# Expert outputs scattered into a table in token order, and the combination in the expert phase

## The reference, cut to what matters

```python
def hier_moe(h, w_rg, b_rg, w_re, b_re, w_up, w_down):
    ...
    top_v, top_i = lax.top_k(logit_e, TOP_K)
    gate = jax.nn.softmax(top_v, axis=-1) * p_grp
    expert = (grp[:, None] * EXPERTS_PER_GROUP + top_i).reshape(-1)
    ...
    def expert_block(args):
        xb, e = args
        g, u = jnp.split(xb @ w_up[e], 2, axis=-1)
        return (jax.nn.silu(g) * u) @ w_down[e]

    y = lax.map(expert_block, (buf.reshape(n_blocks, MOE_BLOCK, D), blk_expert)).reshape(-1, D)
    y = y[dest] * gate.reshape(-1)[order][:, None].astype(h.dtype)
    return jax.ops.segment_sum(y, tok_sorted, num_segments=n_tok)
```

## Time and profile before

| | us |
|---|---|
| median of 3 runs | 2901.03 |
| lowest and highest run | 2896.57, 2902.46 |
| the profiled execution's own time | 2889.24 |
| its span, first to last instruction | 2887.4 |
| TensorE busy in it | 2759.5 |
| VectorE, ScalarE, GpSimd busy in it | 1506.3, 777.0, 79.0 |

### The profile page before, as it was taken

One profiled execution on the slowest core, in us unless ns is written; L12 is line 12 of the kernel. 1 busy time (PEld: TensorE's weight loads), 2 busy tenths in 40 slices (PEclk: granted clock), 3 DMA queues, 4 the chain that ended last, 5 costly groups with the idle time before them and its releaser, 6 DMA issues. The chain is left out here.

```text
span 2887.4 us, 44114 instructions
## 1 busy us (share of the span) xinstructions
PE 2759.5 (96%) x18251; PEld 1644.2 (57%) x18251; DVE 1506.3 (52%) x2115; ACT 777.0 (27%) x1444; POOL 79.0 (3%) x106
## 2 busy tenths in 40 slices
PE   8999889999999999999999989999998899999985
PEld 4444554444444444444454445656564899999974
DVE  7886676566666668773642008856765111111103
ACT  2111771111111115412100016756423121112111
POOL 0000000000000000000000000000000000000022
PEclk9999999999999999999999999999999899999997
DMA  3022842111111127763231000022202999999992
GB/s 143 31 73 40 264 175 73 44 44 44 44 44 44 44 67 280 265 245 111 71 90 44 8 11 1 1 59 88 75 7 75 375 402 406 409 410 405 405 359 79
DMA packets 82614, 422.65 MB, mean 146 GB/s; under 512 B 13504, under 2 KB 23232, under 8 KB 66496
## 3 DMA queue, kind: packets, MB, share of 16 engines
q1 hardware_dynamic: 58528, 362.29, 34.1%
q10 hardware_dynamic: 15664, 41.95, 4.0%
q0 software_dynamic: 8304, 16.79, 1.8%
HBM read 393.07 MB, written 51.38 MB: 154 GB/s over the span
## 5 line engine op out<-in xcount | busy, mean ns | idle before, releaser
L3605 PE MATMUL ex_up_ps<-big,ex_xT 128*32 128x128 f32 x3072 | 349.1, 274 | 0.0
L3603 PE MATMUL ex_up_ps<-big,ex_xT 128*32 128x384 f32 x3072 | 344.8, 490 | 0.7 <-ACT ex_xT L3690 0.6
L3605 PEld LDWEIGHTS ex_up_ps<-big,ex_xT 128*32 128x32 f32 x3072 | 334.3, 110 | 0.6
L1758 PE MATMUL ffn_ps<-h,V 128*128 128x512 f32 x504 | 219.7, 592 | 0.0
L2217 PE MATMUL ffn_ps<-big,V 128*128 128x512 f32 x484 | 211.3, 597 | 3.7 <-DVE V L2472 1.4
L3603 PE MATMUL ex_y_ps<-ex_wd,ex_hT 128*32 128x384 f32 x1536 | 180.9, 493 | 5.1 <-issue 4.3
L296 DVE TENSOR_SCALAR_CACHE_REDUCE h<-ad_s_ps 128x1280 f32<-128x1280 f32 x64 | 92.9, 1489 | 172.7 <-PE ad_s_ps L205 172.7
L3605 PE MATMUL ex_y_ps<-ex_wd,ex_hT 128*32 128x128 f32 x1536 | 178.8, 276 | 3.0 <-issue 2.9
L3605 PEld LDWEIGHTS ex_y_ps<-ex_wd,ex_hT 128*32 128x32 f32 x1536 | 169.0, 111 | 7.2 <-issue 6.5
L1758 PEld LDWEIGHTS ffn_ps<-h,V 128*128 128x128 f32 x504 | 95.8, 190 | 120.5 <-issue 120.5
L2217 PEld LDWEIGHTS ffn_ps<-big,V 128*128 128x128 f32 x484 | 92.2, 191 | 120.4 <-issue 114.5
(11 more groups left out here) (603 smaller groups left out, 4799.0 us busy)
## 6 DMA issues: line engine op xcount, KB each, us to landing
big<-in_w_eup SPq DMA_DIRECT2D x64, 2048.0 KB, 20.9
ex_wd<-in_w_edown SPq DMA_DIRECT2D x32, 2048.0 KB, 20.7
V<-in_w_down SPq DMA_DIRECT2D x35, 704.0 KB, 5.6
dn_tail<-in_w_mod ACTq DMA_DIRECT2D x48, 512.0 KB, 5.4
fm_up<-in_w_up SPq DMA_DIRECT2D x22, 1028.0 KB, 4.9
y_dram<-in_cos SPq DMA_DIRECT2D x1, 21504.0 KB, 71.5
y_dram<-big ACTq DMA_DIRECT2D x32, 288.0 KB
dn_tail<-in_w_in SPq DMA_DIRECT2D x17, 512.0 KB, 4.6
```

Source lines behind the costliest of these rows:

```text
L1758: mm = nc.tensor.matmul(bank(i, j), wj[:, k, :], bj[:, k, :], start=(k == 0), stop=(k == 3))
L3603: nc.tensor.matmul(o[32 * g:32 * g + 32, 0:W], rows(g), w[:, 0:W], start=first, stop=last)
L3605: mm = nc.tensor.matmul(o[BR:P, g * P:(g + 1) * P], rows(g), w[:, W:BANK], start=first and g == 0, stop=last and g == GR - 1)
```

## The change

`y_dram` becomes a table of 2T = 2048 rows in token order: half 0 holds for each token the row of its expert with the lower number, half 1 the other. The fill of `y_dram` and ScalarE's wait for it go. In the routing, VectorE makes for each row its place in the table (`code`, five instructions, and one more for the ids), and `early`, `late` and their eleven instructions go.

In the expert loop the two stores of a block become three DMAs from SBUF to SBUF on ScalarE's queue (32 KB each), which bring the last 256 columns beside the others, and one indirect DMA on GpSimd's queue, which scatters the 96 rows of 4 KB into the table. GpSimd waits for the three, issues the scatter, and waits for the scatter before it goes on; `keep_y` waits for GpSimd's count `y_free`. The scatters of pair i-1 stand behind the two gathers in iteration i.

At the end there are no gathers: SyncE loads the table as 16 plain tiles of 512 KB, half 0 once the scatter of the last block but one is done, half 1 once the last is. The combination is part of the same phase. Four tiles go through TensorE as before, for the other four ScalarE scales the first expert's rows, and VectorE adds them to the residual, which it makes from the rows that the routing left in `V` times their root mean square (`std`). VectorE makes the gates at the start of the expert phase (`weigh`, ten instructions; the gates are exchanged where the halves are).

```diff
@@ dilated_attention
-                sp.dma_start(y_dram.rearrange("(b p) n -> p b n", p=P),
-                             din["cos2"].unsqueeze(1).to_broadcast([P, NB * BR // P, T])).then_inc(y_filled, 16)
@@ route, VectorE
+                st.done(V_.tensor_tensor(swapped, first_at, c1, ALU.is_gt))
+                for a in range(2):
+                    st.done(V_.tensor_scalar(code[:, a], swapped, float(T) * (1 - 2 * a), float(T) * (a - 2), ALU.mult, ALU.add))
+                    st.done(V_.tensor_tensor(code[:, a], code[:, a], cst["token"], ALU.add))
...
-                V_.tensor_scalar(r["ids"][0:BR, 0:NB], ids_ps[0:BR], float(T), None, ALU.add).then_inc(ids_kept, 1)
+                st.done(V_.tensor_scalar(flag[0:BR], ids_ps[0:BR], -float(T), -float(T), ALU.is_ge, ALU.mult))
+                V_.scalar_tensor_tensor(out=r["ids"][0:BR, 0:NB], in0=ids_ps[0:BR], scalar=2.0 * T, in1=flag[0:BR], op0=ALU.add,
+                                        op1=ALU.add).then_inc(ids_kept, 1)
+                V_.tensor_scalar(r["rows"][0:BR, :], ids_ps[0:BR], 2.0 * T, None, ALU.add)
@@ experts, SyncE
+                for f, got, a in ((f0, got0, 0), (f1, got1, 1)):
+                    sp.wait_ge(up_done, pairs * 2 + (a + 1))
+                    sp.wait_ge(y_free, pairs * 2 + (a + 1))
+                    for t in (4, 0, 5, 1, 6, 2, 7, 3) if a == 0 else range(TT):
+                        sp.dma_start(f[:, t, :], y_dram[a * T + t * P:a * T + (t + 1) * P, :]).then_inc(got[t], 16)
...
@@ experts, GpSimd
+                def scatter(i, u):
+                    nc.gpsimd.tensor_copy(row_at[0:BR, u:u + 1], r["rows"][0:BR, bass.ds(i * 2 + u, 1)]).then_inc(row_set, 1)
+                    pool.wait_ge(row_set, i * 2 + (u + 2))
+                    pool.sem_inc(pool_seen, 1)
+                    pool.wait_ge(moved[u], i * (16 * GR) + 16 * GR)
+                    pool.sem_inc(pool_seen, 1)
+                    pool.indirect_dma_start(y_dram, bass.IndirectOffsetOnAxis(ap=row_at[0:BR, u:u + 1], axis=0), y[0:BR, u, :], None,
+                                            bounds_check=2 * T - 1, oob_is_err=False).then_inc(stored[u], 16)
+                    pool.wait_ge(stored[u], i * 16 + 16)
+                    pool.sem_inc(y_free, 1)
...
                         pool.wait_ge(turned, i * 2 + 1)
                         gather(i, 1, i * 2)
                         pool.wait_ge(turned, i * 2 + 2)
                         gather(i + 1, 0, i * 2 + 1)
+                        scatter(i - 1, 0)
+                        scatter(i - 1, 1)
...
-                        pool.indirect_dma_start(f[:, t, a, :], None, y_rows,
-                                                bass.IndirectOffsetOnAxis(ap=r["early"][:, a, t:t + 1], axis=0),
-                                                bounds_check=NB * BR - 1, oob_is_err=False).then_inc(got[t], 16)
+                scatter(pairs - 1, 0)
+                scatter(pairs - 1, 1)
@@ experts, TensorE, behind down(pairs - 1, 1)
+                token_sum(0)
+                token_sum(1)
+                token_sum(2)
+                pe.wait_ge(y_kept, pairs * 2 + 1)
+                token_sum(3)
@@ experts, ScalarE
-                    act.dma_start(dst[:, 0:2 * W], y[0:BR, u]).then_inc(stored[u], 16)
-                    act.dma_start(dst[:, 2 * W:D].rearrange("(g p) n -> p g n", g=GR),
-                                  y[BR:P, u].rearrange("p (g n) -> p g n", g=GR)).then_inc(stored[u], 16)
+                    for g in range(GR):
+                        act.dma_start(y[32 * g:32 * g + 32, u, 2 * W:D], y[BR:P, u, g * 2 * P:(g + 1) * 2 * P]).then_inc(moved[u], 16)
...
+                for t in range(PET, TT):
+                    act.wait_ge(got0[t], 16)
+                    nc.scalar.activation(f0[:, t, :], f0[:, t, :], ACT.Copy, scale=r["gate"][:, 0, t:t + 1]).then_inc(scaled, 1)
@@ experts, VectorE
                 def keep_y(i, u):
                     dve.wait_ge(y_done, i * 2 + (u + 3))
-                    dve.wait_ge(stored[u], i * (16 * PARTS) + 16 * PARTS)
+                    dve.wait_ge(y_free, i * 2 + (u + 1))
...
+                for t in range(PET, TT):
+                    dve.wait_ge(scaled, t - PET + 1)
+                    row = rows[:, t % ROWS, :]
+                    nc.vector.scalar_tensor_tensor(out=row, in0=row, scalar=r["std"][:, t:t + 1], in1=f0[:, t, :], op0=ALU.mult,
+                                                   op1=ALU.add).then_inc(added, 1)
```

More of the change, by code:

```diff
@@ L3161, in route @@
         g4b, begun = carve(TT, 4), carve(E_)
-        c1, low, pg = (carve(TT) for _ in range(3))
+        c1, low, pg, first_at = (carve(TT) for _ in range(4))
+        code = carve(2, TT)
+        std, swapped = r["std"], r["swapped"]
         base, nblk, incl, onesr, total = (carve(E_) for _ in range(5))
@@ L3461, in _ @@
                                              ALU.is_equal))
-                    st.done(V_.scalar_tensor_tensor(out=here, in0=wide(cst["token"], NB), scalar=-float(T), in1=here,
-                                                    op0=ALU.add, op1=ALU.mult))
+                    st.done(V_.tensor_tensor(here, wide(code[:, a], NB), here, ALU.mult))
                     V_.tensor_tensor(lanes[:, a * TT:(a + 1) * TT, 0:BR], wide(lanef[:, a], BR),
@@ L3520, in experts, with used_pairs @@
             "y_kept"))
+        gates_ready, summed, scaled, added, mixed, squared, rooted, inverted, finished, step = (ph.sem(x) for x in (
+            "gates_ready", "summed", "scaled", "added", "mixed", "squared", "rooted", "inverted", "finished", "step"))
         def used(eng):
             return eng.value_load(r["count"][0:1, 0:1], min_val=1, max_val=NB)
+        def used_pairs(eng):
+            return eng.value_load(r["count"][0:1, 1:2], min_val=1, max_val=NB // 2)
         with nc.Block() as block:
@@ L3552, in _ @@
                         load_down(i, 0, i * 2)
-                pairs = sp.value_load(r["count"][0:1, 1:2], min_val=1, max_val=NB // 2)
+                pairs = used_pairs(sp)
                 load_down(pairs - 1, 1, pairs * 2 - 1)
+                for f, got, a in ((f0, got0, 0), (f1, got1, 1)):
[3 more added lines that the diff above has]
+                        sp.dma_start(f[:, t, :], y_dram[a * T + t * P:a * T + (t + 1) * P, :]).then_inc(got[t], 16)
+                for t in range(TT):
+                    sp.wait_ge(finished, t + 1)
+                    sp.dma_start(out[t * P:(t + 1) * P, :], f1[:, t, :]).then_inc(out_stored, 16)
+                sp.wait_ge(out_stored, 16 * TT)
             @block.gpsimd
@@ L3651, in down, with token_sum @@
                     mm.then_inc(y_done, 1)
+                def token_sum(t):
+                    for k in range(KD):
+                        nc.tensor.matmul(sum_ps[t][:, k // 4, k % 4 * P:(k % 4 + 1) * P], h[:, k, t * P:(t + 1) * P], cst["ident"],
+                                         start=(k % 4 == 0), stop=False)
+                    pe.wait_ge(got0[t], 16)
+                    for half in range(2):
+                        mm = nc.tensor.matmul(sum_ps[t][:, half, :], r["diag"][:, t, :], f0[:, t, half * BANK:(half + 1) * BANK],
+                                              start=False, stop=True)
+                    mm.then_inc(summed, 1)
                 turn(0, 0)
@@ L3777, in _ @@
                         keep_y(i, 0)
[L3778 removed]
+                pairs = used_pairs(dve)
                 keep_hidden(pairs - 1, 1)
@@ new lines, in _ @@
+                for t in range(PET, TT):
[3 more added lines that the diff above has]
+                                                   op1=ALU.add).then_inc(added, 1)
+                def mix(t):
+                    if t < PET:
+                        dve.wait_ge(summed, t + 1)
+                        rest = sum_ps[t].rearrange("p a n -> p (a n)")
+                    else:
+                        dve.wait_ge(added, t - PET + 1)
+                        rest = rows[:, t % ROWS, :]
+                    dve.wait_ge(got1[t], 16)
+                    nc.vector.scalar_tensor_tensor(out=f1[:, t, :], in0=f1[:, t, :], scalar=r["gate"][:, 1, t:t + 1], in1=rest,
+                                                   op0=ALU.mult, op1=ALU.add).then_inc(mixed, 1)
@@ L3913, in experts_block @@
         x_ready = [nc.alloc_semaphore("x_ready0"), nc.alloc_semaphore("x_ready1")]
-        f = big[:, 0:16, :].rearrange("p (t a) n -> p t a n", a=2)
-        got = [nc.alloc_semaphore(f"got{t}") for t in range(TT)]
         with nc.sbuf_tensor("wb", [P, KD, 2 * P], F32) as wb:
```

219 lines of the change are left out of this document (75 added, 144 removed).

## The result

The changed kernel takes 3055.39 us (3047.32 to 3064.18, 4 runs), beside 2899.24 us (2896.57 to 2902.46, 4 runs) for the kernel before: 1.0545 times as long, 95% interval 1.0524 to 1.0565. The forecast was 3020 us in a range of 2925 to 3065. The sign, the place and the range were right; 35 us of loss were not foreseen.

The account below looks back on a forecast made before the run. TensorE, busy 96% of the span, was taken as the bound. Loop waits +152.6, tail -33.4 and +0.2 on 2889.24 us gave 3008.6; with 11.8 for the median, 3020 us, range 2925 to 3065.

Parts of the forecast that it names:

- The bound and the ring: Expert loop: turn(i+1,1) waits for a gather queued behind scatter and moves, 8.8 us late, 14 times; full wait's chance 0.70.
- The ring's length: Expert loop, from the start of `keep_y` to the landed gather: 31.2 us needed, 22.4 us allowed.
- The 1.7 us taken off: Expert loop: the last 3.3 us of the gather see an empty weight queue, so 32.9 us become 31.2.
- the scale of the medians: Whole kernel: the median of the runs is 11.8 us above the profiled execution, so 3008.6 becomes 3020 us.
- The rest at nothing: Fill, routing and gates outside loop and tail: removed or added work costs nothing, except +0.2 us before the ids.
- Loaded, not quiet: Expert loop: transfers take loaded durations, gather and scatter 10.3 us each and moves 9.5, instead of 3.8 and 3.3 quiet.
- the second rival: Expert loop: the chain fits (10.8 us by the skill's rule), only the tail counts, 2868 us; chance 0.09 with engines' bound.
- One packet in turn: DMA queues in the loop: engines take a packet from each queue in turn, so fewer queued weights don't shorten the chain.
- The clock: Expert loop, behind each wait: TensorE runs some 4.3 us at half speed, losing 2.1 us, 14 times.
- The tail: From the start of down(15,0) to the end: 62.3 us instead of 95.7, -33.4 us; bounds -16 and -40.
- The first rival's sum: Expert loop: the ring waits less, 3 to 7.5 us a pair, 42 to 105 us, 2922 to 2985; chance 0.18.
- The third rival: Expert loop: DMA engines become the bound, 0.3 us more per block, 2878 us; chance 0.09 together with the fitting chain.

Follow-up runs that it names:

- e2_order: The changed kernel with the next iteration's gathers queued ahead of the scatter of block (i-1,1): 2864.72 us, in a later set 2868.97 us.
- b1: The kernel before, with GpSimd issuing its 16 early gathers only after the last down product: 2900.58 us, ratio 1.0010.
- c_before_b: The kernel before, unchanged, run again in a later set: its own run 2876.35 us, the kernel's median there 2867.23 us.
- c_after_b: The changed kernel, unchanged, run again beside the kernel before at 2867.23 us: 3054.30 us, ratio 1.0651.

## Why the prediction was right, and where it was short

- **The bound and the ring.** Right. The wait is where the prediction put it, 14 times, at turn(i,1), with the gather queued behind a scatter that is queued behind moves; e2_order removes the loss by order alone.
- **The ring's length.** 31.2 us forecast, 34.0 measured, and this is the term that was mis-sized. The 1.7 us taken off, for weights that would end near 29.6, was wrong: in the changed kernel weight packets still ran 32 us after that `keep_y`, through most of the gather, which took its loaded time (10.8 us for 10.3). A weight load lands in 10.5 us, not in the some 7 that I worked out from 400 GB/s and a start. The moves took 12.1 us to the scatter instead of 9.5 + 0.5; the scatter 9.2 instead of 10.3. Together 2.8 us per pair, 14 x 2.8 = 39 us: more than the whole 35 of the miss. The full balance: the loop 40.5 more than forecast (193.1 for 152.6), the tail 1.0, the stretch ahead of the loop 6.9, and 13.3 less by the scale of the medians (under "The rest at nothing").
- **Loaded, not quiet.** Right, and now tested: with half the weight bytes the ring fits. The Trainium skill's fixed cost plus bytes at 436 GB/s ("DMA: Bandwidth & Descriptors", anatomy of one DMA), the second rival, gives 2.9 us for a transfer that took 9 to 11 here. Half the weight bytes brought the scatter to 5.0.
- **One packet in turn.** From the rule of the Trainium skill that each queue gives a packet in turn (same page, queues, rings and completion order) the prediction drew that a shorter backlog of weights would not shorten the chain. That held roughly: after the change weights land in 10.5 us instead of 21 and the gathers in 8.9 in the median instead of 10.2; in e2_order, with weight loads landing in 24.7, they take 11.8. The row that the prediction gave for the rule does not show it: 103 weight packets ahead of the store's first are over six on each of 16 DMA engines. What speaks for it is what follows, once the store runs (before, 2583 to 2587 us), nearly as many packets of the one queue as of the other (packets, MB, share of 16 engines):

```profile
q1 hardware_dynamic: 104, 1.51, 88.1%
q10 hardware_dynamic: 102, 0.19, 12.0%
```

- **The clock.** 2.1 us a pair forecast, some 2.3 in the trace, and 2.1 given back in the mean when the wait was filled.
- **The tail.** 62.3 us forecast, 63.2 measured from the same point. The lower bound of 16 us rested on the stretch being a coincidence in time; b1 speaks for the gathers as its cause, and c_before_b shows that they don't cause it always. Against the kernel before where it takes 2867 us the tail gains only some 7 us (from the `keep_y` of (14,1) 81.9 there, 74.6 in the changed kernel), and the loss is 187 us (c_after_b) instead of 156. One trace could not show this, and which of the two times the kernel before would have in the comparison was luck.
- **The rest at nothing.** Nothing in the runs speaks against it. The 11.8 us for the scale of the medians was about right on the kernel before (10.0 by the four runs); for the changed kernel the profiled run was already at its median (3056.9 to 3055.4). That this term was 13.3 too high hid a third of the loop's miss, by luck.
- **The first rival's sum.** 42 to 105 us on top of 2868 are 2910 to 2973, not the 2922 to 2985 that it states: the 11.8 us were added twice. The forecast doesn't hang on it.
- **The third rival.** In e2_order the DMA share is 1.02, and the blocks are 17.00 all the same. It did not bind.

## What to carry to other kernels

Where one engine issues both a store of results and the load of a coming block, draw the ring through that queue and compare it with the slack in time, with durations from loaded rows; busy shares (3% here) don't show it. Put the load whose inputs are known early ahead of the store that must wait for fresh results: the same transfers in another order were worth 185 us. And don't credit a chain with quiet time later on unless you have seen where the competing transfer lands.

## What was not expected of the hardware

- The kernel before runs at 2867 or at 2898 us for a whole set of runs, at mean granted clocks that overlap (0.979 to 0.985 in the set at 2868.5, 0.974 to 0.982 in the one at 2896.8), and two thirds of the difference lie in one down product with gathers beside it.
- A granted clock that fell in a wait of 11.5 us could be kept at 1.00 by matmuls of no use, and 195 of them made the kernel 21 us faster than itself. With gaps of 2 to 4 us left at the turns the clock fell in nine of fourteen pairs and little came back, and without the moves it fell to 0.50 behind a gap of 2.07 us.
- Gathers that were allowed to overlap with a scatter of the same queue landed in 15.6 us in the median, where they landed in 8.9 when they were issued after its landing.
